# Differential attention: scores in three passes over split queries and keys, in place of full fp32 products

## The reference, cut to what matters

```python
Q_BLOCK, CHUNK, DIFF_HEADS, DIFF_HEAD_DIM = 128, 64, 8, 64
def block(args):                      # i: one of 8 blocks of 128 queries
    q_i, i = args
    mask = key_chunk[None, :] <= q_chunk[:, None]          # chunks of 64 tokens
    sc = jnp.einsum('bqhtd,bkhtd->bhtqk', q_i, kf) * scale # t = 2 maps, d = 64, fp32
    p = jax.nn.softmax(jnp.where(mask, sc, neg), axis=-1)
    w = p[:, :, 0] - lam * p[:, :, 1]
    return jnp.einsum('bhqk,bkhe->bqhe', w, vf)
```

## Time and profile before

| | |
|---|---|
| median of 3 runs | 3028.28 us (3028.24 to 3034.36) |
| the profiled execution's own time | 3034.68 us |
| its span, first to last instruction | 3033.0 us |
| PE busy | 2831.1 us (93%) |
| DVE, ACT busy | 1609.2 us (53%), 655.8 us (22%) |
| mean granted TensorE clock | 0.984 |
| differential attention, first score to last output | 2336.9 to about 2915 us, 8 heads |

### The profile page before, as it was taken

One profiled execution on the slowest core, in us unless ns is written; L12 is line 12 of the kernel. 1 busy time (PEld: TensorE's weight loads), 2 busy tenths in 40 slices (PEclk: granted clock), 3 DMA queues, 4 the chain that ended last, 5 costly groups with the idle time before them and its releaser, 6 DMA issues.

```text
span 3033.0 us, 35236 instructions
## 1 busy us (share of the span) xinstructions
PE 2831.1 (93%) x13336; PEld 2229.2 (73%) x13336; DVE 1609.2 (53%) x2059; ACT 655.8 (22%) x1157; POOL 291.6 (10%) x287
## 2 busy tenths in 40 slices
PE   6889999989999999998999999999998999999996
PEld 4757766867878787776888888888766777777664
DVE  5655445354554545546544454544464666666644
ACT  3133334031111111112110110011032333333321
POOL 0589800000000000000000000000000000000000
PEclk9999999999999999999999999999999999999998
DMA  3211111324343334333222222222232222222121
GB/s 146 84 56 56 52 45 41 127 105 145 112 156 133 138 135 155 139 110 139 71 82 83 83 70 85 80 81 71 84 148 102 70 75 77 73 69 70 52 111 69
DMA packets 48617, 286.59 MB, mean 94 GB/s; under 512 B 6576, under 2 KB 6704, under 8 KB 18608
## 3 DMA queue, kind: packets, MB, share of 16 engines
q1 hardware_dynamic: 22064, 119.01, 11.4%
q0 software_dynamic: 14544, 105.91, 10.2%
q10 hardware_dynamic: 11952, 60.89, 5.2%
HBM read 248.03 MB, written 29.36 MB: 91 GB/s over the span
## 4 chain that ended last, share of the span: by engine, by line
PE 75%; DVE 15%; issue 5%; ACT 3%; DMA 2%; DVEq 0%; SPq 0%; ACTq 0%
PE PB L238 11%; PE PB L240 11%; PE PB L239 11%; PE OBB L238 8%; PE OBB L240 8%; PE OBB L239 8%; PE OBB L841 3%; PE TBB L753 3%; PE PB L799 3%; PE TBB L238 2%; PE TBB L240 2%; PE TBB L239 2%; DVE small L1009 1%; DVE V L1532 1%; DVE WL L254 1%
## 5 line engine op out<-in xcount | busy, mean ns | idle before, releaser
L238 PE MATMUL PB<-HH,WH 128*128 128x512 f32 x1520 | 600.5, 395 | 24.5 <-issue 7.6
L240 PE MATMUL PB<-HH,WL 128*128 128x512 f32 x1520 | 595.2, 392 | 0.0
L239 PE MATMUL PB<-HL,WH 128*128 128x512 f32 x1520 | 595.2, 392 | 0.0
L238 PE MATMUL OBB<-HH,WH 128*128 128x512 f32 x992 | 400.6, 404 | 5.6 <-DVE WL L254 5.5
L240 PE MATMUL OBB<-HH,WL 128*128 128x512 f32 x992 | 388.0, 391 | 0.0
L239 PE MATMUL OBB<-HL,WH 128*128 128x512 f32 x992 | 387.6, 391 | 0.0
L238 PEld LDWEIGHTS PB<-HH,WH 128*128 128x128 f32 x1520 | 287.8, 189 | 92.3 <-issue 28.0
L239 PEld LDWEIGHTS PB<-HL,WH 128*128 128x128 f32 x1520 | 287.9, 189 | 61.9 <-issue 2.2
L240 PEld LDWEIGHTS PB<-HH,WL 128*128 128x128 f32 x1520 | 287.4, 189 | 60.5
L254 DVE TENSOR_TENSOR WL<-RAW,WH 128x2048 fp32r<-128x2048 f32 x101 | 233.4, 2310 | 57.1 <-DMA WH<-units 39.4
L2051 POOL DMA_DIRECT2D WH<-units x85 | 45.5, 535 | 2075.5 <-PE PB L238 1350.6
(11 more groups left out here) (314 smaller groups left out, 3754.4 us busy)
## 6 DMA issues: line engine op xcount, KB each, us to landing
WH<-units POOLq DMA_DIRECT2D x85, 1024.0 KB, 5.0
RAW<-units SPq DMA_DIRECT2D x85, 1024.0 KB, 4.7
gs<-units ACTq DMA_DIRECT2D x16, 1024.0 KB, 4.8
gu<-gs ACTq DMA_DIRECT2D x16, 1024.0 KB, 3.9
RAW<-gu SPq DMA_DIRECT2D x16, 1024.0 KB, 4.8
WH<-gu POOLq DMA_DIRECT2D x16, 1024.0 KB, 5.2
tmpd<-xr SPq DMA_DIRECT2D x128, 64.0 KB, 2.0
A<-xT SPq DMA_DIRECT2D x4, 1024.0 KB, 12.7
```

The source lines that it names most:

```text
L238: first = pe.e.matmul(out, wh, xh, start=start, stop=False)
L239: pe.e.matmul(out, wh, xl, start=False, stop=False)
L240: return pe.e.matmul(out, wl, xh, start=False, stop=stop), first
```

## The change

The prepared queries and keys of the differential attention are split, as activations are elsewhere. `qT` and `kT` aren't used there any more. ACT writes the high parts `qh` (from the same scaled copy) and `kh`. DVE writes the low parts `ql` and `kl` in a new function `low_scores`, which takes the place of the copy kT<-kN. `scores` issues three F32R matmuls for each map and 512 keys, over at least 256 columns. PE waits for `ck` (now ACT's) and `kl`. `ql` and `kl` lie where nothing lives at that time (the space of xr7, and tile 7 of A).

```diff
@@ -793,7 +797,16 @@
-                for b in range(0, n, HALF):
+                for b in range(0, n if not forget else 0, HALF):
+
+                    w = max(256, min(HALF, n - b))
+                    for q_part, k_part in ((qh, kh), (qh, kl), (ql, kh)):
+                        for c in range(2):
+                            rows = slice(64 * c, 64 * c + 64)
+                            pe.e.matmul(PB[c][:, b:b + w], q_part[rows, t * P:(t + 1) * P],
+                                        k_part[rows, b:b + w], start=q_part is qh and k_part is kh,
+                                        stop=False, skip_group_check=True)
+                for b in range(0, n if forget else 0, HALF):
@@ -863,8 +876,8 @@
-                pe.e.wait_ge(act_done, at_last(pe, "act", "cq", i))
-                pe.e.wait_ge(dve_done, at_last(pe, "dve", "ck", i))
+                pe.e.wait_ge(act_done, at_last(pe, "act", "cq" if forget else "ck", i))
+                pe.e.wait_ge(dve_done, at_last(pe, "dve", "ck" if forget else "kl", i))
             scores(0)
@@ -996,7 +1009,11 @@
-                e.activation(qT[:, :], qN[:, :], ACT.Copy, scale=0.125).then_inc(act_done, act.mark("cq"))
+                e.activation((qT if forget else qh)[:, :], qN[:, :], ACT.Copy, scale=0.125).then_inc(
+                    act_done, act.mark("cq"))
+                if not forget:
+                    e.wait_ge(dve_done, at_mark(act, "dve", "k1T", i))
+                    e.activation(kh[:, :], kN[:, :], ACT.Copy).then_inc(act_done, act.mark("ck"))
@@ -1084,9 +1101,21 @@
-                e.wait_ge(dve_done, at_mark(dve, "dve", "Nk1" if forget else "k1T", i))
-                e.tensor_copy(kT[:, :], kN[:, :]).then_inc(dve_done, dve.mark("ck"))
+                if forget:
+                    e.wait_ge(dve_done, at_mark(dve, "dve", "Nk1", i))
+                    e.tensor_copy(kT[:, :], kN[:, :]).then_inc(dve_done, dve.mark("ck"))
+                else:
+                    low_scores(dve, i)
                 low_part(dve, u0 + 4, i, 2)
+
+        def low_scores(dve, i):
+
+            dve.e.wait_ge(act_done, at_mark(dve, "act", "cq", i))
+            dve.e.scalar_tensor_tensor(ql[:, :], qN[:, :], 0.125, qh[:, :].bitcast(F32),
+                                       ALU.mult, ALU.subtract).then_inc(dve_done, dve.mark("ql"))
+            dve.e.wait_ge(act_done, at_mark(dve, "act", "ck", i))
+            dve.e.tensor_tensor(kl[:, :], kN[:, :], kh[:, :].bitcast(F32),
+                                ALU.subtract).then_inc(dve_done, dve.mark("kl"))
```

More of the change, by code:

```diff
@@ L722, in build @@
         kN = work("kN", [P, S], F32, 12 * K)
+        qh = work("qh", [P, S], F32R, 0)
+        kh = work("kh", [P, S], F32R, 4 * K)
+        ql = at("ql", [P, S], F32R, 108 * K)
+        kl = at("kl", [P, S], F32R, 28 * K)
         vF = work("vF", [P, S], F32, 16 * K)
@@ L1156, in first_act @@
             act.e.wait_ge(dve_done, at_mark(act, "dve", "Nq1" if forget else "q1T"))
-            act.e.activation(qT[:, :], qN[:, :], ACT.Copy, scale=0.125).then_inc(act_done, act.mark("cq"))
+            act.e.activation((qT if forget else qh)[:, :], qN[:, :], ACT.Copy, scale=0.125).then_inc(
+                act_done, act.mark("cq"))
             if not forget:
+                act.e.wait_ge(dve_done, at_mark(act, "dve", "k1T"))
+                act.e.activation(kh[:, :], kN[:, :], ACT.Copy).then_inc(act_done, act.mark("ck"))
                 act.e.wait_ge(pe_done, at_mark(act, "pe", "rtok"))
@@ L1177, in first_dve @@
                         taps(dve, range(*{("q", 0): (12, 14), ("q", 1): (14, 15), ("k", 0): (15, 16)}[x, h]))
-            dve.e.wait_ge(dve_done, at_mark(dve, "dve", "Nk1" if forget else "k1T"))
-            dve.e.tensor_copy(kT[:, :], kN[:, :]).then_inc(dve_done, dve.mark("ck"))
+            if forget:
+                dve.e.wait_ge(dve_done, at_mark(dve, "dve", "Nk1"))
+                dve.e.tensor_copy(kT[:, :], kN[:, :]).then_inc(dve_done, dve.mark("ck"))
+            else:
+                dve.e.wait_ge(spilled, 16 + 64)
+                low_scores(dve, None)
             low_part(dve, u0 + 2)
```

## The result

The changed kernel takes 3039.52 us (median of 8 runs, 3035.96 to 3049.21), the kernel before beside it 3030.33 us (8 runs, 3028.08 to 3034.36). The medians are 9.2 us apart. The ratio of the runs is 1.0036, with a 95% interval of 1.0022 to 1.0050, which is 7 to 15 us. The prediction was 3037.8 us, 9.5 us above the 3028.3 us known then. The profiled execution took 3048.07 us, one of the two longest of the eight; its span is 3046.4 us and its mean granted clock 0.983. Times are therefore compared as medians, and the profile is read for the length of its parts.

A forecast was written before the change was run, and what follows sets the result against it. PE was taken to bound blocks 0 to 4, DVE from block 5's maxima on. Bodies +6.8, first head +1.9, last head -1.2 and clock +2 gave +9.5 us on 3028.3: 3037.8 us, 8-in-10 range 3028 to 3056.

The forecast's parts named there:

- The length of the scores: Scores in each block: three F32R passes, maps side by side and loads hidden, in total -1.20 us a head.
- B: Scores: F32R products of the two maps don't run side by side; +48 us, 3076 us; chance 0.12.
- C: Scores: weight loads show between a map's passes, 0.108 us each; +25 us, 3053 us; chance 0.07.
- What of it counts: Scores in a body: blocks 1 to 5 count, 0.69 us; block 0 and blocks 6 and 7 count nothing.
- PE never waits in blocks 0 to 4: Blocks 0 to 4 of a body: DVE and ACT wait for PE, so each microsecond of scores counts.
- blocks 6 and 7 count for nothing: Blocks 6 and 7 of a body: shorter scores only lengthen PE's waits for DVE ahead of the values.
- The late output: End of a body: ql and kl on DVE delay the normalised output, so PE's ot transposes start 1.66 us later.
- The wait for ACT: End of a body: DVE's ql waits for ACT's qh, 0.7 us.
- First head: Prologue: ql and kl replace the copy kT, +1.73 us, and scores(0) adds +0.13; together +1.9 us.
- Last head: Last head: PE waits for DVE's weights, which hang on the scores, so all blocks count; -1.2 us.
- The sum: Whole kernel: seven bodies +6.8 us, first head +1.9 and last head -1.2, together +7.5 us before the clock.
- The clock: PE's new pauses at ends of bodies: half-clock stretches of 3.4 us, one in five at most; +2 us.

The follow-up runs named there:

- e3: The changed kernel with fp32 products of qh and kh back in blocks 6 and 7 of the seven bodies; 3042.4 us, body 74.02 us.
- e8: Kernel with output first and prologue low parts moved earlier, plus the late low part of weights in block 3, not 4; 3027.3 us, body 72.70.
- e4: The changed kernel with ACT's copies qh and kh moved ahead of the silu and its table loads; 3033.3 us, body 73.25 us.
- e2: The changed kernel with the splitting kept but scores as fp32 products of qh and kh; 3045.5 us, body 74.50 us.
- e5: The changed kernel with one constant matmul more ahead of PE's wait for the normalised output in each body; 3040.0 us, body 74.04 us.
- e1: The changed kernel without low parts: three F32R passes of qh by kh, waits and copies as before the change; 3024.5 us, body 72.43 us.
- e6: The changed kernel with ql, kl and kh made behind the normalised output at the end of a body; 3025.5 us, body 72.47 us.
- e10: The kernel of e6 with all three products of map 0 issued before those of map 1; 3028.3 us, body 72.50 us.
- e9: The kernel of e6 without the floor of 256 columns, so some products have 128; 3026.9 us, body 72.40 us.

## Why the prediction was right, step by step

- **The length of the scores.** Forecast for blocks 1 to 5, in order: -0.09, -0.13, -0.17, -0.04, -0.26 us. Measured in the second body from first score to mask, after less before: -0.09, -0.14, -0.16, -0.02, -0.24. The maps run side by side and loads are hidden: cases B and C didn't occur. The three products of one map, all on the same 64 rows of the array, start 0.23 us apart at 512 columns and 0.12 at 256. Half the columns take half the time, which leaves no room for a load of 0.11 in each. That the maps run side by side in fp32 too, which I assumed for the forecast, shows in the trace of the kernel before: each fp32 product is two records there (x4 for one product of each map), in block 5 those of the two maps start less than 0.01 us apart, and 128 more keys cost both maps together 0.213 us, where one fp32 product of 128 columns over all 128 rows takes 0.22 (16 records of L841 at 0.11 us each). How many passes an fp32 product takes inside, no row shows.
- **What of it counts.** The term of 0.69 us a body was too large; it measured 0.54. Most of the difference is block 1's gain: the projection behind it goes into the bank from which DVE takes the first half of the gate, and can't start before that is done. In the second body before, L1031 ends at 2417.97 us and the projection starts at 2418.02; with the scores alone it starts as late after the `ot` transposes (9.88 us in both), and 0.38 us behind the start of block 0's values, for 0.29 before. I had said that PE never waits in blocks 0 to 4, and overlooked this pause, which is too short for the listing to name its cause. That blocks 6 and 7 count for nothing held (e3). That DVE's backlog alone is the reason didn't (e8).
- **The late output.** Forecast +1.66 us a body; measured +1.53 with the split alone, and 1.08 + 0.54 = 1.62 with both. The normalised output starts 2.47 us later behind the output of block 7, forecast 2.49. The wait for ACT in it, forecast 0.7 us, is 0.80 (e4).
- **First head**: forecast +1.73 us from rotation to score, measured 1.67, and 1.62 in the other kernels with the same first head.
- **Last head**: forecast -1.2 us. Its blocks shrank by what the scores did: from the transposes of block 5 to those of block 6 it is 7.43 us before, with the earlier trace rows as its start, and 7.14 after. From the transposes of block 0 to those of block 7 of this head it is 47.25 us before and 46.11 after, -1.1.

```profile
2900.86 0.87 PE L757 MATMUL TBB<-con,E 128*128 128x128 f32 x6 [1.48 <-DVE E L1041]
2908.00 1.07 PE L757 MATMUL TBB<-con,E 128*128 128x128 f32 x7 [1.53 <-DVE E L1041]
```

- **The sum.** 7 x 1.08 + 1.67 + 0.12 (scores(0) of the first head) - 1.1 = +8.3 us; the medians say +9.2, with an interval of 7 to 15. The forecast had 7.5 for these parts and 2 for the clock. That 9.5 came within 0.3 us of 9.2 is luck in part: the gain of the scores was 0.15 us a body too large, the clock term made up for it, and the medians don't resolve either.
- **The clock.** The term of 2 us takes 3.4 us at half clock behind at most one gap in five. No run shows that rate for the ends of bodies; it comes from the feed-forward loop of the kernel before, where PE pauses for 2.1 us in five places. Over the 6 us around them the granted clock is 1.00 at four, and 0.72 at the fifth, that is 3.4 us at 0.50. That the pause is the cause isn't shown. At the ends of bodies the profiles have 3 in 21 with the new gap (below). The medians of the change leave 0.9 us for the term, less than they resolve. The profiles show that such stretches do come behind the new gap. In the seven bodies the kernel before has none at half clock (0.50). The change, e2 and e3, in which PE stands for 1.4 us ahead of the `ot` transposes, have one each, 1.7 to 2.3 us behind the start of these transposes. The change has one more, behind the first score. In this order, the change at the first score and at the last body's end, then e2, then e3:

```profile
2340.30:2343.70 3.40, 3.40 (x13) 2.81 (x11) 1.70 (x6) 1.78 (x6) 0.00 (x0) 0.50 0.42 125
2859.10:2865.90 6.80, 6.09 (x24) 5.22 (x25) 1.79 (x6) 1.89 (x6) 0.00 (x0) 0.50 0.19 81
...
2784.00:2787.40 3.40, 3.40 (x12) 3.02 (x13) 1.04 (x5) 2.00 (x6) 0.00 (x0) 0.51 0.15 60
...
2856.70:2860.10 3.40, 3.24 (x17) 2.98 (x18) 1.06 (x6) 1.45 (x6) 0.00 (x0) 0.52 0.19 80
```

That is 3 of 21 ends of bodies with a gap of 1.4 us. Of the 7 with the gap filled to 0.5 us (e5), the 7 with 0.6 us (e4) and the 49 without (before, e1, e6 to e10) none has one. In e2 it makes the body 76.20 us, for 74.50. From the lengths, 13.6 us at half clock in three executions, I estimate some 2.3 us for each, the size of the forecast term. The medians less the sum of their parts leave 0.9 us for the change, 4.7 for e2, 5.9 for e3, 2.3 for e4 and 2.2 for e5, and -1.2 to 1.0 for the six kernels (e1, e6 to e10) in which PE doesn't wait for the output. So something beyond the parts is lost where it waits. That it is the clock alone isn't shown: three stretches are few, and e4 and e5 lose as much without one in their profiles. The two stretches of the change make its profiled execution some 5 us longer. The one behind the first score is also in the profiles of e9 and e10, whose first score comes as late as in the change; it is in 3 of the 8 profiles where it does, and in none of the other 4.

## What to carry to other kernels

A product that gets cheaper is worth only what the blocks in which PE sets the pace let through: here 0.54 us of 1.2 a body. The preparation that it needs is paid where it stands in another engine's queue: 2.5 us more on DVE, work and wait for ACT together, cost PE 1.5 to 1.6 ahead of the operation that it wanted next, and next to nothing behind it. So before giving up such a change, look for the place in the queue where the engine waits anyway; here that turned 9 us lost (7 to 15) into 4 us won (1 to 7).

## What the runs showed of the hardware that I had not expected

- Products on the two halves of the array's rows paired up in both orders of issue that were tried. With three of map 0 ahead of three of map 1, the pairs still start 0.23 us apart and a body takes 72.50 us, against 72.47.
- F32R products of 128 columns didn't fall back to the pace of fp32 (e9). They start 0.12 us apart, as those of 256 do, where fp32 needs 0.213 for 128 columns, 3.7 times the 0.057 that the F32R products of 512 columns take for 128 of them. Their weight loads start 0.11 us apart; I take these to set the pace, but no run varied them.
- An F32R product of 512 columns costs 0.23 us. An fp32 one costs 0.85, four times the 0.213 of 128 columns, in two records whose starts are 0.43 apart. So three F32R products are 0.69 for 0.85, 19% less.
